# Convolution taps dealt by whole rounds, rope angles computed earlier, the layer norm's first load split and moved up

## The reference, cut to what matters

```python
mod = c @ w_ada + b_ada
shift, scale, gate = split(mod, 3)
h = rmsnorm(x, norm_g) * (1.0 + scale) + shift
proj = h @ w_in            # glu_a, glu_b, z_conv, q, k, v (24 heads of 64 each), z_att, g_conv, g_att
u = glu_a * sigmoid(glu_b)
u = depthwise_causal_conv(u, conv_w, 31 taps) + conv_b       # 1024 channels
u = silu(layernorm(u, conv_ln_g, conv_ln_b))
y_conv = (u * silu(z_conv)) @ w_conv_out
q, k = partial_rope(q, positions), partial_rope(k, positions)  # 16 of 64 features, cos and sin
# three groups of 8 heads: windows 128, 512, 2048 with dilations 1, 4, 16, combined by their softmax weights
att = combine(dilated_attention(q, k, v))
y_att = (att * silu(z_att)) @ w_att_out
x = x + gate * ((sigmoid(g_conv) * y_conv + sigmoid(g_att) * y_att) @ w_o)
x = rmsnorm(x, final_g)
...                         # second block: pooling, sliding window attention, MLP of 4096
```

## Time and profile before

| | us |
|---|---|
| median of 3 runs | 2697.19 (2696.49 to 2697.64) |
| the profiled execution, its own time | 2698.34 |
| its span, first to last instruction | 2696.5 |
| PE busy | 2611.0 (97%) |
| DVE busy | 1389.3 (52%) |
| POOL busy | 888.3 (33%) |
| mean granted clock of PE | 0.989 |

### The profile page before, as it was taken

The page is one execution under the profiler, slowest core; times in us unless marked ns, Lnnn a source line. Parts: engine busy times, 40 slices in busy tenths (PEclk is TensorE's granted clock), DMA queues, the critical chain, the costliest instruction groups (busy, mean ns, idle before and its releaser), DMA issues.

```text
span 2696.5 us, 32948 instructions
## 1 busy us (share of the span) xinstructions
PE 2611.0 (97%) x12400; PEld 2180.0 (81%) x12400; DVE 1389.3 (52%) x2410; ACT 605.0 (22%) x1392; POOL 888.3 (33%) x870
## 2 busy tenths in 40 slices
PE   7999999999999998979999999999999999999997
PEld 4787889978899887757888888878878888888886
DVE  5611349877688675683664511226354343433436
ACT  4213221123211222530132132321131101010102
POOL 3422213422343232242344222232233333333334
PEclk9999999999999999989999999999999999999998
DMA  7311221222312234432342032243331111111113
GB/s 243 98 47 52 70 74 36 68 72 79 113 47 64 77 103 147 146 124 88 131 145 85 27 108 73 67 138 130 109 111 48 47 47 47 51 51 51 50 54 125
DMA packets 148707, 231.82 MB, mean 86 GB/s; under 512 B 22499, under 2 KB 63203, under 8 KB 148581
## 3 DMA queue, kind: packets, MB, share of 16 engines
q1 hardware_dynamic: 147428, 225.94, 26.5%
q10 hardware_dynamic: 1152, 4.19, 0.4%
HBM read 179.55 MB, written 50.53 MB: 85 GB/s over the span
## 4 chain that ended last, share of the span: by engine, by line
PE 81%; DVE 12%; DMA 3%; issue 2%; ACT 1%; POOL 1%; SPq 0%; POOLq 0%; DVEq 0%; ACTq 0%
PE ps L1932 47%; PE ps L2140 13%; PE ps L2174 12%; DVE scr L1446 4%; PE ps L2051 3%; PE ps L2027 2%; PE ps L2037 2%; PE ps L1961 1%; DMA raw<-in_w_in 1%; POOL w_lo L938 1%; DMA scr<-o_d 1%; PE ps L1974 1%; DVE act_lo L1325 1%; DMA scr<-in_x 1%; DVE big L1575 1%
## 5 line engine op out<-in xcount | busy, mean ns | idle before, releaser
L936 POOL CAST w_hi<-raw 128x512 fp32r<-128x512 f32 x416 | 302.1, 726 | 1740.9 <-DMA raw<-in_w_in 780.2
L938 POOL TENSOR_TENSOR w_lo<-raw,w_hi 128x512 fp32r<-128x512 f32 x416 | 576.0, 1385 | 33.3
L1932 PE MATMUL ps<-act_hi,w_hi 128*128 128x512 f32 x1344 | 541.9, 403 | 24.2 <-DVE scr L1458 9.4
L1932 PE MATMUL ps<-act_lo,w_hi 128*128 128x512 f32 x1344 | 535.9, 399 | 0.0
L1932 PE MATMUL ps<-act_hi,w_lo 128*128 128x512 f32 x1344 | 528.8, 393 | 0.0
L1446 DVE SCALAR_TENSOR_TENSOR scr<-scr,small 128x512 f32<-128x512 f32 x480 | 429.7, 895 | 15.6
L1932 PE MATMUL ps<-w_hi,act_hi 128*128 128x512 f32 (+1 forms) x960 | 384.9, 401 | 0.9 <-POOL w_lo L938 0.9
L1932 PE MATMUL ps<-w_hi,act_lo 128*128 128x512 f32 (+1 forms) x960 | 374.1, 390 | 0.0
L1932 PE MATMUL ps<-w_lo,act_hi 128*128 128x512 f32 (+1 forms) x960 | 374.1, 390 | 0.0
L1932 PEld LDWEIGHTS ps<-act_hi,w_hi 128*128 128x128 f32 x1344 | 255.1, 190 | 86.6 <-issue 14.8
L1932 PEld LDWEIGHTS ps<-act_lo,w_hi 128*128 128x128 f32 x1344 | 254.7, 189 | 57.6 <-issue 4.6
(11 more groups left out here) (188 smaller groups left out, 2758.9 us busy)
## 6 DMA issues: line engine op xcount, KB each, us to landing
raw<-in_w_in SPq DMA_DIRECT2D x176, 256.0 KB, 3.2
raw<-in_w_up SPq DMA_DIRECT2D x64, 256.0 KB, 2.7
raw<-in_w_down SPq DMA_DIRECT2D x64, 256.0 KB, 2.6
vreg<-in_w_ada SPq DMA_DIRECT2D x48, 256.0 KB, 3.4
raw<-in_w_in SPq DMA_DIRECT2D x72, 128.0 KB, 2.3
x_d<-big SPq DMA_DIRECT2D x16, 512.0 KB, 3.0
scr<-x_d SPq DMA_DIRECT2D x16, 512.0 KB, 4.2
o_d<-scr SPq DMA_DIRECT2D x48, 128.0 KB, 2.1
```

The lines of the kernel that those rows point to most:

```text
L936: pool.tensor_copy(dhi, src).then_inc(w_hi_done, 1)
L938: pool.tensor_tensor(dlo, src, dhi.bitcast(F32), ALU.subtract).then_inc(w_ready, 1)
L1932: ins = nc.tensor.matmul(out_, lhs, rhs, start=(m == 0), stop=(m == 3 * nk - 1))
```

## The change

Three things.

1. `tap_plan`. Before, 38 taps lay in the last 38 steps of attention 0, 5 a unit in projection 1 (120), 2 a step in attention 1 (128), 4 a unit in projection 2 (96), and the last 114 in the first 57 steps of attention 2. Now 31 lie in the last 31 steps of attention 0; projection 1 has 124 (4 or 5 in the q and k units, 7, 7, 7, 6, 6, 6, 6, 7 in the v units); each attention 1 and 2 has 124 (8, 8, 8, 7 in each four rounds, through the last round); projection 2 has 93 (4 a unit, 3 in the eighth). So a half tile ends with a unit or a round everywhere: behind q6, k5, v2 and v7 in projection 1, behind rounds 3, 7, 11 and 15 in attention 1 and 2, behind q7, k7 and v7 in projection 2.
2. The second half of h's affine step is written behind the angles.
3. The norm stage's first load of `cb` is made in two halves of four channel tiles, with a semaphore of its own for the second (`cb0_ld`), and stands first on SP: it waits for `c_d`'s stores and the attention's end alone. The two pieces of `prefetch_z(0)` stand behind it, and the waits for the other stores behind those. The second transposing unit `ct(0,1)` waits for the second half.

```diff
-    give([("step", 0, s) for s in range(26, 64)], 1)
-    give([(t, 1, B) for t in "qkv" for B in range(NB)], 5)
-    give([("step", 1, s) for s in range(64)], 2)
-    give([(t, 2, B) for t in "qkv" for B in range(NB)], 4)
-    give([("step", 2, s) for s in range(64)], 2)
+    def quads(g):
+        give([("step", g, s) for s in range(64)], ([2] * 15 + [1]) * 4)
+
+    give([("step", 0, s) for s in range(33, 64)], [1] * TAPS)
+    give([(t, 1, B) for t in "qkv" for B in range(NB)],
+         [5, 4, 5, 4, 5, 4, 4] * 2 + [5, 5] + [7, 7, 7] + [6, 6, 6, 6, 7])
+    quads(1)
+    give([(t, 2, B) for t in "qkv" for B in range(NB)], ([4] * 7 + [3]) * 3)
+    quads(2)
...
             def conv_block(B):
-                if B > 0:
-                    wait_unit(sp, ("lt", B - 1, 1))
-                sp.dma_start(cb.rearrange("p (k s) -> p k s", k=KT),
-                             c_d.rearrange("(k p) s -> p k s", p=P)[:, :, P * B:P * B + P]).then_inc(cb_ld, 16)
+                dst = cb.rearrange("p (k s) -> p k s", k=KT)
+                src = c_d.rearrange("(k p) s -> p k s", p=P)[:, :, P * B:P * B + P]
+                if B == 0:
+                    sp.dma_start(dst[:, 0:4], src[:, 0:4]).then_inc(cb_ld, 16)
+                    sp.dma_start(dst[:, 4:8], src[:, 4:8]).then_inc(cb0_ld, 16)
+                    return
+                wait_unit(sp, ("lt", B - 1, 1))
+                sp.dma_start(dst, src).then_inc(cb_ld, 16)
...
+            sp.wait_ge(c_st, 16 * 16)
+            sp.wait_ge(pv, 16 * NG)
+            conv_block(0)
             prefetch_z(0)
-            sp.wait_ge(c_st, 16 * 16)
             for n in range(2):
                 sp.wait_ge(ob_st[n], OB_TOTAL[n])
             sp.wait_ge(stat_st, 16 * 4)
+            for g in range(NG):
+                sp.dma_start(sg[:, g], st_d[g].rearrange("(b p) c -> p b c", p=P)).then_inc(sg_ld, 16)
+            attention_block(0)
             for t in range(4):
                 for h in range(2):
                     wait_stored(sp, ("za", t, h))
-            sp.wait_ge(pv, 16 * NG)
-            conv_block(0)
-            for g in range(NG):
-                sp.dma_start(sg[:, g], st_d[g].rearrange("(b p) c -> p b c", p=P)).then_inc(sg_ld, 16)
-            attention_block(0)
             sp.dma_start(attzT, gate_d["za"].rearrange("(k p) s -> p k s", p=P)).then_inc(za_ld, 16)
...
-            mod_half(1)
-            for k in range(4, KT + 1):
-                ...
             freq = np.float32(THETA) ** (-(np.arange(8, dtype=np.float32) * np.float32(2.0 / 16)))
...
+            mod_half(1)
+            for k in range(4, KT + 1):
+                ...
...
                 if name == "ct":
                     pe.wait_ge(cb_ld, 16 * (B + 1))
+                    if (B, h) == (0, 1):
+                        pe.wait_ge(cb0_ld, 16)
```

More of the change, by code:

```diff
@@ L349, in build @@
         stat_st, stat_free = sem("stat_st"), sem("stat_free")
-        cb_ld, ln_var, ln_sd, ln_rs, ln_un = (sem(n) for n in ("cb_ld", "ln_var", "ln_sd", "ln_rs", "ln_un"))
+        cb_ld, cb0_ld, ln_var, ln_sd, ln_rs, ln_un = (sem(n) for n in ("cb_ld", "cb0_ld", "ln_var", "ln_sd", "ln_rs", "ln_un"))
         o_ld, cmb_m, cmb_e, att_done, za_ld = (sem(n) for n in ("o_ld", "cmb_m", "cmb_e", "att_done", "za_ld"))
@@ L1414, in _ @@
                 nc.vector.tensor_scalar(dst, dst, 3.1415925, -3.1415925, ALU.min, ALU.max).then_inc(ang_ready, 1)
+            mod_half(1)
+            for k in range(4, KT + 1):
+                if k < KT:
+                    h_affine(k)
+                if k >= 5:
+                    h_lo(k - 1)
             def rotate(u, heads):
```

9 lines of the change are left out of this document (2 added, 7 removed).

## The result

| | before | after |
|---|---|---|
| median of 6 runs each, us | 2697.34 | 2708.24 |
| lowest and highest | 2695.07 to 2702.26 | 2704.92 to 2709.98 |
| ratio after to before | | 1.0031 (95%: 1.0020 to 1.0043) |
| the profiled execution, its own time | 2698.34 | 2705.22 |
| its span | 2696.5 | 2703.3 |

By the ratio the change costs 8.4 us; the two profiled executions lie 6.8 us apart, and these 6.8 are what the traces can account for. The profiled execution of after is the second fastest of its six.

The account below looks back on a forecast made before the run. PE, busy 97% of the span, bounds the kernel. Opening -2.7, group 1 +2.4, projection 2 -0.4, attention 2 -0.8 and norm stage +4.3 make +2.8 on 2696.5, 2699.3, plus 0.7 for the median: 2700.0 us, range 2691 to 2706.

Parts of the forecast that it names:

- half clock in group 1: Upper bound, +5 us, for projection 1 and attention 1: a slow PE spell behind the long wait, not taken up by round 1.
- The likeliest case: Whole kernel: the change measures the same, between 2691.8 and 2702.6 us; chance 0.62.
- Opening: Start to 150 us: PE's wait for the first rotated q block goes, about 2 us return near 111; -2.7 us (-4.3 to -1.4).
- Group 1: Projection 1 and attention 1: DVE's tap debt moves to attention 1's start, round 4's wait goes; +2.4 us (-2 to +5).
- The rival of a smaller debt: Before attention 1: DVE ends its taps at 551 again, giving -1.5 instead of +2.4, total 2696 us; chance 0.20.
- Projection 2: Second projection stage: with 93 taps for 96, a 0.8 us wait may go or be replaced; -0.4 us (-0.8 to +0.8).
- Attention 2: Last attention stage: round 12's wait falls by 0.8, rounds 13 and 14 add none; -0.8 us (-2.5 to +0.5).
- Norm stage: Its start: the last taps' store delays the first half of `cb`, PE stands 6.2 to 6.8 us; +4.3 us (+2.5 to +7.7).
- the rival in which the late pieces cost more than `cb`: Norm stage: late weight pieces set the fifth gate unit, 7.7 us lost instead of 4.3, total 2703.4 us; chance 0.25.
- All waits go and none takes their place: Whole kernel: PE's waits in opening, group 1 and attention 2 vanish, norm stage +2.9; -11, 2686 us; chance 0.12.

Follow-up runs that it names:

- e_angles: Kernel before with only the angles moved ahead of the second half of h's affine step; ratio to before 0.9987.
- v_early: Changed kernel with 93 taps in attention 0 and in projection 1, none in rounds 12 to 15 of attention 2; ratio to before 0.9973.
- e_taps: Kernel before with only the new deal of taps, old angles and loads; ratio to before 1.0055.
- e_short15: Changed kernel without the last seven taps of the last half tile (round 15 of attention 2), so its convolution is incomplete; ratio to before 1.0009.
- e_last: Changed kernel with no taps in rounds 12 to 15 of attention 2, 31 more in attention 0, 124 kept in projection 1; ratio to before 0.9987.
- v_even: Changed kernel with 93 taps in attention 0 and projection 1, none in attention 2's rounds 12 to 15, spread evenly; ratio to before 0.9955, median 2689.11 us.
- e_debt31: Changed kernel with 31 taps moved from projection 1 (now 93) to attention 0 (now 62); ratio to before 0.9998.
- v_even_oldload: Changed kernel with evenly spread taps, 93 in attention 0, none in attention 2's rounds 12 to 15, and the old norm-stage loads; ratio to before 0.9962.

## Why the prediction was right, and where it was not

The forecast was +2.8 us on the span; the traces show +6.8 and the ratio 8.4, so the direction was right and the size a third to two fifths of what came. The predicted 2700.0 us is 8.2 under the median after and 5.5 under what the ratio makes of the 2697.19 (2705.5), which is just inside the range of 2691 to 2706; the median of after itself, 2708.24, lies above it. That the range holds the 2705.5 is partly luck: its upper end came from late pieces of weights in the norm stage and half clock in group 1, and of these only the second was seen. The likeliest case, a change too small to tell (0.62), did not come; a slower kernel by over 0.2% had a chance of 0.25. Point by point:

- **Opening: right, at its other bound.** Everything behind the gate row came 3.1 us earlier (shift -3.1 at 115), PE stands 1.71 us where 2 were forecast, and of the two cases the one with half clock behind it came: -1.4, the bound named for it. e_angles has the same. In v_early the same wait (1.72 us) has full clock behind it (1.00 from 112.0 to 115.5), and the shift is -2.7 at 150: the other case.
- **Group 1: right in mechanism; that the size fits is partly luck** (+2.4, measured +2.6). The last 31 taps took 29.8 us for 29.9, PE's wait was 5.92 us for 5 to 6, and round 4's wait went. The step's own terms, added up, would have given a wait of 7 us (555 + 2.0 less 550); PE's first `turn_four` came 1.26 us behind the first `score_max` and not 2.0. The term that was put at nothing in the sum is the clock: the long wait brought 6.8 us at half clock, PE busy in 4.0 of them, so about 2 us, which the forecast had only in its upper bound. e_taps, e_short15 and e_last have the same 124 taps in projection 1, a long wait (6.28, 5.89 and 6.60 us) and 6.8 us at half clock too, and give +4.3, +4.6 and +5.0; the +2.6 is the lowest of the four. q2's wait is 0.50 us where 1.5 was forecast, and 0.78, 1.65 and 0.89 in those three. The rival of a smaller debt is refuted.
- **Projection 2: wrong, -0.4 forecast (to +0.8), +1.4 measured.** q2's rotation is late, a wait of 1.28 us at 751.67. The text left open whether the small wait goes or is replaced; it was added to. e_angles, with the old deal, loses 0.9 there too, so at most part of it is the deal's. v_even, with 3, 3, 3 taps in the first units, has no wait there; what sets this one stays open.
- **Attention 2: the step that failed.** -0.8 forecast, with bounds -2.5 and +0.5; measured +2.7, the largest miss. Round 12's wait went, as its more favourable bound had it (shift 0.0 at 1020). But the step then says that round 13 "keeps its 8" and that round 14's "fit, to within 0.5". They did not: PE waits 1.77, 2.55 and 0.85 us in rounds 13 to 15. The step gave the taps one price and left POOL out, which it had reckoned with in group 1. It also passed over a wait that the kernel before had there, of 1.41 us in round 14 (1041.02 above): round 13's eight taps were too many even with POOL at rest, so there was no room for more. The windows show the longer rows of taps (first after, then before; POOL's busy time is the fifth pair):

```profile
1020.20:1029.30 9.10, 8.84 (x47) 6.81 (x46) 8.85 (x9) 0.00 (x0) 7.62 (x6) 1.00 0.33 102
1035.60:1043.00 7.40, 6.41 (x33) 4.68 (x31) 7.15 (x10) 0.00 (x0) 2.74 (x2) 1.00 0.21 71
1046.40:1055.10 8.70, 8.70 (x48) 7.05 (x47) 8.45 (x10) 0.00 (x0) 4.72 (x4) 1.00 0.20 60
```

```profile
1018.20:1027.00 8.80, 8.80 (x44) 7.04 (x43) 8.55 (x10) 0.11 (x1) 4.85 (x4) 0.88 0.20 60
1033.20:1039.50 6.30, 6.30 (x33) 4.68 (x31) 6.05 (x10) 0.00 (x0) 0.00 (x0) 1.00 0.00 2
```

  Round 12's last seven taps run beside three pieces and take 9.07 us; before, all eight ran beside two, in 8.66, and PE, at half clock until 1020.4 there (0.88 over the window), did not wait behind them; now it is at full clock. Round 13's eight run beside one piece and take 7.40, 1.14 more than before, when they ran alone in 6.26, and PE's wait behind them grew by the same 1.14, from 1.41 to 2.55. Round 14's eight run beside two and take 8.71, where there were two taps before. The store of the finished half tile now stands at the end of round 11, and SP issued three pieces behind it, at 1017.18, 1018.66 and 1020.13, so that their splits fell into the row of taps that follows. That POOL makes the rows longer is read from these windows; no run moved the pieces alone. That the taps in these rounds make the waits is shown by e_last. Between after and e_last, which has no taps in these rounds, lie 2.7 + 4.8 = 7.5 us in this stage.
- **Norm stage: right** (+4.3 forecast, +3.8 measured, and +3.7 in e_debt31). The chain is the one forecast: last tap, store 2.55 us (2.5 forecast), half of `cb` 3.17 us (3.2), PE's wait 6.23 us (6.2 to 6.8), the spell at half clock twice as long, 6.8 us. e_short15 confirms the cause. Behind 1121 us 2.1 come back, since PE then waits less for DVE (for L1458, now L1464, 9.4 us in all before and 6.5 now); the forecast had no such term, and the rival in which the late pieces cost more than `cb` did not come.
- **All waits go and none takes their place** (0.12) did not come with this deal. The waits themselves were real, though: with the taps elsewhere group 1 gives -7.0 and attention 2 -4.8.

That the measured gap by the ratio (8.4) is 1.6 wider than in the two traces is left open; it is within the interval (5.4 to 11.6). The sister traces point at luck in the profiled execution of after: besides group 1, e_taps and e_short15 have 3.4 us and e_debt31 has 6.8 us at half clock behind these waits of attention 2 (windows at 0.50 from 1033.5, 1034.3 and 1036.4), and after has none.

## What to carry to other kernels

- Filler work on an engine that feeds the bound engine needs a place where that engine has room, not an even border. Count, for each stage, the filler's time at the price that it has beside its neighbours (here 0.79 us a tap alone, 1.1 to 1.4 where POOL splits pieces beside it), and look where the debt comes due: moved, it shows up at the next stage's start.
- The last piece of filler has a deadline: what is loaded from its result. Finish it before the stage's last rounds, and then the order of the loads matters little (v_even against v_even_oldload).
- A load moved ahead takes the place of the ones behind it. Ask which transfer is late next before counting the wait that goes.
